# Moving the attention's row subtraction from VectorE to GpSimd in blocks 2 to 4

## What is computed

```
sp_next = concatenate([softplus(z)[..., 1:], 0])          # z: scaled logits, strictly causal
suffix  = cumsum(sp_next, reverse=True)
w       = exp(log_sigmoid(z) - suffix)
out     = w @ v
```

```
act = gelu(einsum('ckd,cd->ck', expert_u[idx], x))
y   = einsum('ck,ckd->cd', gate * act, expert_v[idx])
```

## Time and profile before

| | |
|---|---|
| median of 3 runs | 3343.8 us (3340.32 to 3344.42) |
| profiled execution | 3340.76 us |
| its span | 3339.0 us |
| VectorE busy | 2134.4 us, 64% |
| TensorE busy | 2612.4 us, 78%, mean granted clock 0.897 |
| ScalarE busy | 1085.5 us, 33% |
| GpSimd busy | 1200.5 us, 36% |
| moved by DMA | 1280.42 MB, of these 1073.81 MB in gathers |

### The profile page before, as it was taken

One profiled execution on the slowest core, in us unless ns is written; L12 is line 12 of the kernel. 1 busy time (PEld: TensorE's weight loads), 2 busy tenths in 40 slices (PEclk: granted clock), 3 DMA queues, 4 the chain that ended last, 5 costly groups with the idle time before them and its releaser, 6 DMA issues.

```text
span 3339.0 us, 40432 instructions
## 1 busy us (share of the span) xinstructions
PE 2612.4 (78%) x14560; PEld 1335.0 (40%) x14560; DVE 2134.4 (64%) x4998; ACT 1085.5 (33%) x3411; POOL 1200.5 (36%) x1049
## 2 busy tenths in 40 slices
PE   8998888998888778987878777998785555555555
PEld 6776534564444344552444333553351111111111
DVE  2324669776567987775458888675448656765444
ACT  2112344342332642323223552332322222223222
POOL 0001333333333443342433444333334444444443
PEclk9998999999999999999899989999988877777777
DMA  4357999999999999999999999999999999999997
GB/s 134 113 158 261 417 388 342 403 405 412 417 417 417 415 396 417 418 416 417 418 414 404 400 364 418 418 418 415 418 410 408 419 417 421 417 417 411 421 421 325
DMA packets 226839, 1280.42 MB, mean 383 GB/s; under 512 B 25168, under 2 KB 27216, under 8 KB 95568
## 3 DMA queue, kind: packets, MB, share of 16 engines
q0 software_dynamic: 147456, 1073.81, 78.4%
q1 hardware_dynamic: 64272, 162.09, 13.3%
q10 hardware_dynamic: 14912, 41.95, 3.2%
HBM read 1260.97 MB, written 16.78 MB: 383 GB/s over the span
## 4 chain that ended last, share of the span: by engine, by line
DMA 39%; PE 32%; DVE 15%; issue 6%; ACT 5%; POOL 3%; ACTq 0%; POOLq 0%; DVEq 0%; SPq 0%
DMA rowsb<-uv,e_idx 38%; PE yacc L893 13%; PE mixp L590 7%; DVE rowsb L1699 6%; POOL rowsb L963 3%; PE mixp L602 2%; PE mixp L641 2%; ACT diag L1261 2%; DVE area L1353 2%; ACT wg L1256 2%; PE mixp L652 1%; PE mixp L615 1%; PE yacc L590 1%; DVE area L1385 1%; ACT gmt L1242 1%
## 5 line engine op out<-in xcount | busy, mean ns | idle before, releaser
L963 POOL DMA_INDIRECT rowsb<-uv,e_idx x1024 | 1195.9, 1168 | 2111.2 <-PE yacc L893 1649.8
L1699 DVE CUSTOM_DVE_ANT_0 rowsb<-rowsb,hnrow 128x1024 f32<-128x1024 f32 x1024 | 1241.0, 1223 | 837.6 <-DMA rowsb<-uv,e_idx 825.1
L893 PE MATMUL yacc<-rowsb,diag 64*64 64x512 f32 x8192 | 1222.1, 721 | 675.9 <-ACT diag L1261 661.0
L893 PEld LDWEIGHTS yacc<-rowsb,diag 64*64 64x64 f32 x8192 | 299.5, 150 | 1419.0 <-ACT diag L1261 985.0
L1242 ACT ACTIVATE gmt<-dots 128x2 f32<-128x2 f32 x512 | 104.1, 203 | 1735.8 <-DVE dots L1699 1721.4
L590 PE MATMUL mixp<-area,wt 128*128 128x256 f32 x2144 | 496.1, 385 | 1.2 <-ACT area L1035 1.2
L590 PEld LDWEIGHTS mixp<-area,wt 128*128 128x128 f32 x2144 | 399.3, 191 | 128.0 <-issue 78.3
L1261 ACT ACTIVATE diag<-ident,wg 128x64 f32<-128x64 f32 x1024 | 300.4, 340 | 16.7
L1256 ACT ACTIVATE wg<-gmt,gate 128x1 f32<-128x1 f32 x1024 | 245.5, 286 | 17.7
L981 ACT ACTIVATE area<-mixp 128x512 f32<-128x512 f32 (+3 forms) x334 | 147.9, 486 | 282.1 <-PE mixp L590 169.9
L615 PE MATMUL mixp<-area,wt 128*128 128x256 f32 x960 | 230.5, 395 | 4.4 <-DMA wt<-w_query_ 4.1
(11 more groups left out here) (214 smaller groups left out, 1785.6 us busy)
## 6 DMA issues: line engine op xcount, KB each, us to landing
wt<-w_merge SPq DMA_DIRECT2D x96, 512.0 KB
wt<-w_feat SPq DMA_DIRECT2D x80, 512.0 KB
wt<-w_query_ SPq DMA_DIRECT2D x64, 512.0 KB
wt<-w_tok SPq DMA_DIRECT2D x32, 512.0 KB
wt<-w_out_ SPq DMA_DIRECT2D x32, 512.0 KB
rowsb<-uv,e_idx POOLq DMA_INDIRECT x1024
area<-x_rows ACTq DMA_DIRECT2D x4, 1024.0 KB, 12.5
area<-keysT ACTq DMA_DIRECT2D x16, 256.0 KB, 11.2
```

The lines of the kernel that those rows point to most:

```text
L893: last = pe.matmul(yacc[at:at + HP, k % 2, c * NCH:(c + 1) * NCH], diag[r * HP:(r + 1) * HP, s, :], rowsb[r * HP:(r + 1) * HP, s, D + c * ...
L963: pool.indirect_dma_start(rowsb[:, n % RS, :], None, uv, bass.IndirectOffsetOnAxis(ap=e_idx[:, i % 2, k:k + 1], axis=0)).then_inc(row_load ...
L1699: dve.tensor_tensor_reduce(rowsb[:, s, 0:D], rowsb[:, s, 0:D], hnrow[:, i % 2, :], 1.0, 0.0, ALU.mult, ALU.add, dots[:, s:s + 1]).then_inc ...
```

## The change

In blocks 2 to 4 the subtraction is taken from VectorE's `scan` and given to GpSimd. GpSimd gets its own tick generator, `mix(b)`, which walks the same table: after the second gather of slot s + 3 it does the subtractions of the ticks of slot s. VectorE's scan raises a new semaphore, `scan_ready`, which GpSimd waits for; GpSimd's subtraction raises `wts_ready`, which TensorE's flip waits for as before. `left` becomes two rows, used in turn, and from the third row on VectorE's scan waits until the subtraction of the row two before is done. VectorE no longer waits for the end of its scan. The planner's cost of a scan for VectorE falls from 3.2 to 2.1 ns a column in these blocks. Block 1 is unchanged.

```diff
-        left = cut(A_MLQ + 4 * T, T + 8)
+        lefts = [cut(A_MLQ + 4 * T, T + 8), cut(A_EXT, T + 8)]
...
-                    dve_ += 0.58 + 3.2e-3 * (NT * b + queries[v][1] + 1) * P
+                    dve_ += 0.58 + (3.2e-3 if b == 0 else 2.1e-3) * (NT * b + queries[v][1] + 1) * P
...
+                def mix(b):
+                    rem, lefts, wT, span = SBA_AREA[b]
+                    for k in range(N_NORM + N_PROJ1):
+                        yield
+                    for k in range(n_sba(b)):
+                        for v, h in scans_at(b, k):
+                            m = (NT * b + queries[v][1] + 1) * P
+                            left = lefts[(2 * v + h) % 2]
+                            pool.wait_ge(scan_ready, 2 * (NV * (b - 1) + v) + h + 1)
+                            pool.tensor_tensor(rem[:, (2 * v + h) % 4, 0:m], left[:, span - m + 1:span + 1],
+                                               left[:, span - m:span], ALU.subtract).then_inc(wts_ready, 1)
+                        yield
+
+                later = [mix(b) for b in range(1, NB)]
                 for i in range(TT):
                     for k in range(NSEL):
...
+                        s = n // 2 - RS // 2 + 1
+                        if k % 2 == 1 and s >= 0:
+                            for b in range(1, NB):
+                                for _n in range(steps[s][b]):
+                                    next(later[b - 1], None)
...
+                        left = lefts[(2 * v + h) % len(lefts)]
+                        if b > 0 and 2 * v + h >= 2:
+                            dve.wait_ge(wts_ready, 2 * (NV * b + v) + h - 1)
                         back = r_[:, 0:m][:, ::-1]
-                        mark(dve.tensor_tensor_scan(left[:, span - m:span][:, ::-1], back, back, 1.0, ALU.mult, ALU.min))
-                        settle()
-                        dve.tensor_tensor(r_[:, 0:m], left[:, span - m + 1:span + 1], left[:, span - m:span],
-                                          ALU.subtract).then_inc(wts_ready, 1)
+                        ins = dve.tensor_tensor_scan(left[:, span - m:span][:, ::-1], back, back, 1.0, ALU.mult, ALU.min)
+                        if b > 0:
+                            ins.then_inc(scan_ready, 1)
+                        else:
+                            mark(ins)
+                            settle()
+                            dve.tensor_tensor(r_[:, 0:m], left[:, span - m + 1:span + 1], left[:, span - m:span],
+                                              ALU.subtract).then_inc(wts_ready, 1)
...
-                            mark(dve.memset(left[:, span:span + 1], 1.0))
+                            for left in lefts:
+                                mark(dve.memset(left[:, span:span + 1], 1.0))
```

More of the change, by code:

```diff
@@ L165, in build @@
         left_early = early[:, 6 * N:7 * N + 8]
-        SBA_AREA = [(rem_early, left_early, wT_early, N)] + [(rem, left, wT, T)] * (NB - 1)
+        SBA_AREA = [(rem_early, [left_early], wT_early, N)] + [(rem, lefts, wT, T)] * (NB - 1)
         sc = sb("sc", [P, QT, NKEYS])
@@ L209, in build @@
         th_ready, rem_ready, wts_ready = sem("th_ready"), sem("rem_ready"), sem("wts_ready")
+        scan_ready = sem("scan_ready")
         neg_ready, ln_ready, m_ready, em_ready, exp_step = (sem(n) for n in (
@@ L716, in values @@
                         last.then_inc(x_done[bank(("y", b, v))], 1)
-                    rem, left, wT, span = SBA_AREA[b]
+                    rem, lefts, wT, span = SBA_AREA[b]
                     for t in range(NT):
```

## The result

The changed kernel takes 3355.4 us (median of 6), the kernel before 3342.6 us (median of 6): ratio 1.0038, 95% interval 1.0027 to 1.0048. It is slower, by 12.8 us where 28 were forecast. The profiled execution took 3355.24 us, its span is 3353.5 us, the mean granted clock 0.897 as before.

A forecast was written before the change was run, and what follows sets the result against it. The DMA sets 5.03 us a slot, but VectorE bounds the attention of blocks 2 to 4. Added 68 us less removed 41 us gives +27 us: 3368 us beside the profiled 3340.8, 3371 us as median, range 3352 to 3392.

The forecast's parts named there:

- The bound, and what is removed: Attention of blocks 2 to 4: VectorE bounds, the DMA loses 32 us there; 48 subtractions leave VectorE, 41 us.
- no exclusion: Rival: GpSimd's subtraction reads between VectorE's accesses, block 4's slots fall under the DMA's 5.03 us; -22 us, 3322 us; chance 0.20.
- The sum: The three attention stretches: 68 us added on GpSimd, 41 us removed from VectorE, +27 us.
- Exclusion in both directions: VectorE's two-SBUF-input instructions and GpSimd's subtraction take turns, whichever came first, so their times add.
- the price of a subtraction to VectorE: GpSimd's 48 subtractions, two input reads one after the other: 1.42 us each on average, 68 us in all.
- The slot is as long as the sum: Block 4 at 1024 columns: 4.94 us of VectorE plus 1.99 us of GpSimd, 6.9 us where 6.08 stood.
- Two corrections cancel: In the stretches: subtractions falling in VectorE's idle holes save perhaps 4 us; semaphore handing over costs 5 us for 48.
- The planner's lower cost: nothing, ±3 us: Two of block 2's last scan ticks share one slot, block 4's attention moves about one slot: nothing, ±3 us.
- GpSimd's queue order: nothing: Gathers of slot s + 4 behind the subtraction leave 2 to 3 us later, covered by rows on their way: nothing.
- Break-even: Rival: GpSimd's subtraction costs as little as one-input rows, 0.80 us against 0.85 us; 3344 us, ±6; chance 0.09.
- GpSimd becomes the bound: Rival: GpSimd's three jobs a slot each wait for VectorE, 8.6 us a slot in block 4; 3411 us; chance 0.11.

The follow-up runs named there:

- e7_no_subtraction: e1_old_plan with no subtraction at all in blocks 2 to 4, the scan raising the weights' semaphore itself: 3321.6 us, 0.9933 of before; repeated 3323.5 us.
- e3_writes_only: e1_old_plan with each GpSimd subtraction replaced by two writes of zeros, which read nothing: 3325.9 us, 0.9954 of before; repeated 3324.9 us.
- e6_copy_one_input: e1_old_plan with GpSimd copying the scan's row (one SBUF input) in place of the subtraction: 3328.5 us, 0.9955 of before.
- e2_plan_only: The kernel before with only the planner's new scan cost (2.1 ns a column in blocks 2 to 4): 3349.6 us, 1.0026 of before.
- e10_order_alone: e7_no_subtraction, but GpSimd waits for each scan and writes zeros twice into a spare row, ahead of its next gathers: 3324.8 us, 0.9953 of before.
- e1_old_plan: The changed kernel with the planner's old scan cost (3.2 ns a column in all blocks), subtractions still on GpSimd: 3352.1 us, 1.0032 of before.
- e5_subtract_twice: e1_old_plan with GpSimd doing each subtraction twice, once into a spare row: 3408.7 us, 1.0199 of before.

## Why the prediction was half right

**The bound, and what is removed: right, with a cap.** The changed kernel lost its time in the three stretches where the rate had dipped before. But 41 us of VectorE's time were not worth 41: `e7_no_subtraction` gives some 20, as the prediction's rival without exclusion had priced it (22 us), and block 3's slots stood at 5.0 and 5.3 us against the DMA's 5.03. The sum took the removal and the hold in full and netted them, which happens to be sound where the slot stays above 5.03 us on both sides, and is not elsewhere.

**Exclusion in both directions: right.** It was argued from gathers, which show only that GpSimd waits for VectorE. The dots of 2.90 us, `e3_writes_only` and `e6_copy_one_input` show the other direction, that it is the reading, and that its length decides. The rule of the Trainium skill, SBUF — State Buffer, section "Who interferes with whom", agrees with these runs: a VectorE instruction with two SBUF inputs contends with a GpSimd instruction that reads SBUF (a hold of 1.68 us), and not with one that only writes (no hold in `e3_writes_only`).

**The term that was mis-sized, and by which the forecast fell, is the price of a subtraction to VectorE: 68 us in the sum, 46.6 us measured.** "0.17 + 2 · 0.89 ns a column, 1.42 us, 68 us in all" was the subtraction's length, and as that it was nearly exact: the shortest of the changed kernel with 384 columns took 0.82 us, 0.85 by the formula. The Trainium skill, GPSIMD Engine Reference, section "Elementwise — side-by-side cycle accounting", with 4497 ns for 2048 columns (2.2 ns a column), is too high for this trace, where 1024 columns take 1.82 us from the dot's end, 1.78 ns a column; no run here has 2048. But VectorE pays for the hold, not for the length: held were 1.68 us of a forecast 1.99 at 1024 columns, 1.47 of 1.76 at 896. The start (0.17 us) lies inside the dot that still runs; the last 0.1 us of the subtraction doesn't hold the dot either, and why is not shown. Over all rows VectorE's instructions grew by (1283.2 - 1241.0) + (82.4 - 78.0) = 46.6 us, 0.97 us a subtraction and not 1.42. Some 0.3 us of the difference is the start and the end (an estimate: 0.31 at 1024 columns, 0.29 at 896); the rest fell where VectorE was waiting, as here in block 3, where the second dot waits for its rows anyway and is held for 0.21 us only:

```profile
1108.89 1.46 POOL L963 TENSOR_TENSOR area<-area 128x640 f32<-128x640 f32 x1
...
1110.00 1.43 DVE L1728 CUSTOM_DVE_ANT_0 rowsb<-rowsb,hnrow 128x1024 f32<-128x1024 f32 x1 [0.75 <-DMA rowsb<-uv,e_idx]
```

"The slot is as long as the sum", 6.9 us, measured 6.48. 46.6 - 41 leaves +6 us on VectorE in place of +27. With the plan's 2 to 3 us that makes some +9 us, where 12.8 were measured; that 3355 lies inside the prediction's own range, at its lower edge, does not speak for its price of a subtraction.

**"Two corrections cancel": wrong.** I gave 4 us for holes and took 5 us for handing over. There is no handing over to be seen: the held dot ends 1.08 us after the subtraction's end (1895.37 to 1896.45), and its own length is 1.22, so it went on some 0.1 us before that end. The holes and the overlap are worth 68 - 46.6 = 21 us.

**"The planner's lower cost: nothing, ±3 us": wrong for a kernel alone** (+8.5 us, `e2_plan_only`), 2 to 3 us and not resolved on the changed kernel. I had read the two ticks in slot 29 out of the table and priced them by VectorE's load; the slot took 11.2 us in the changed kernel.

**"GpSimd's queue order: nothing": right,** by `e10_order_alone`.

**What stays open.** `e1_old_plan` is 10.9 us over before by the medians (6 to 15 by the interval), and VectorE's balance of holds and removal explains some 6. Seen from the other side: `e7_no_subtraction` is some 20 us under before, so the 46 us of holds cost about 31 us of time. Both steps are worth less than VectorE's time in them, and not by the same share. In the three stretches of the earlier trace rows VectorE is idle for 23 us in `e1_old_plan` where 18 were before (20 if the last two are taken 10 us later), mostly waiting for rows and, at the end of block 2's attention, for TensorE (7.4 us in place of 4.3). Whether this is a consequence of the holds (a held dot delays ScalarE and TensorE, and with them the gathers) was not separated.

Of the rivals, "no exclusion" would have had dots of 1.22 us; it is out. Its time, 3322 us, is near that of `e3_writes_only` (3325.9 and 3324.9), which is the case without reads. "Break-even" gave 3344 us, ±6, and is out by its time; but a price of 0.97 us a subtraction is nearer to its 0.85 than to the forecast's 1.42. "GpSimd becomes the bound" did not come with one subtraction; with two, `e5_subtract_twice`, signs of it did (TensorE's 198 us).

## What to carry to other kernels

Before work goes from VectorE to GpSimd, look what VectorE runs at that time. Here it was instructions with two SBUF inputs, and GpSimd's subtraction, which reads SBUF, didn't run beside them but between them: at 1024 columns it cost VectorE more (1.68 us) than the 1.15 us that the same subtraction took there. GpSimd's instructions that only write ran free. Price the hold (the time of reading) and not the instruction's length, and cap each slot's gain at the DMA's floor before adding up. Where VectorE is the bound, taking the operation out by algebra (differences of the values' inputs once a block in place of differences of every row) gave 26 us where moving it lost 13.

## What the runs showed of the hardware that was not expected

- The engines take turns. With a second subtraction directly behind the first, VectorE still got one instruction in between (the dot, 1926.5 to 1927.5), and then GpSimd went ahead of the triangle, which is shown 1.96 us long.
- A held VectorE instruction is shown as a long one, not as idle time: the 42 us lie in the dots' mean (1223 to 1264 ns), and the waits list no GpSimd releaser for them. Who looks only at idle time doesn't see the loss.
- GpSimd's copy with one input held the dot for 0.83 us at 1024 columns, its subtraction with two for 1.68 us, its writes of the same row not at all.
